# The last expert item of a mixture-of-experts layer taken out of the matmul engine's loop, its scatter products placed between its last products, and the gathered rows added on GpSimd

## What is computed

```
logits = h @ router_w + router_b
top_v, top_i = top_k(logits, 2);  top_p = softmax(top_v)
for e in range(8):                          # D_FF_EXPERT = 2816
    out += gates[:, e:e+1] * ((silu(h @ w1[e]) * (h @ w3[e])) @ w2[e])
x = x + g2 * out
return rmsnorm(x, final_norm_w)
```

## Time and profile before

| | us |
|---|---|
| median of 3 runs | 1505.53 (1504.87 to 1506.3) |
| span of the profiled execution | 1505.1 |
| last item's main products end (chain of waits) | 1493.51 |
| last instruction ends, before the last store lands | 1502.03 |

### The profile page before, as it was taken

How to read it: one execution, slowest core, us unless ns; L and a number is a source line. 1 busy time by engine, 2 the same in 40 slices (tenths; PEclk the granted TensorE clock), 3 DMA queues, 4 the chain that set the end, 5 groups by cost and what they waited for, 6 DMA issues and landing times.

```text
span 1505.1 us, 24325 instructions
## 1 busy us (share of the span) xinstructions
PE 1490.6 (99%) x8505; PEld 1311.0 (87%) x8505; DVE 1299.7 (86%) x1529; ACT 959.8 (64%) x1107; POOL 26.7 (2%) x44
## 2 busy tenths in 40 slices
PE   8999999999999999999999999999999999999997
PEld 7999888999999999888988888888888888888886
DVE  7999787777775799787799999999999999999998
ACT  3636445444544535444588888887878878788885
POOL 0000000000000000000010000000000000000100
PEclk9999999999999999999999999999999999999999
DMA  9956498388995646588399999999999999999993
GB/s 349 341 173 221 151 331 293 103 291 297 377 410 193 210 154 218 174 291 306 109 398 397 410 394 404 372 379 409 363 392 369 382 406 364 393 369 379 411 393 139
DMA packets 210458, 470.89 MB, mean 313 GB/s; under 512 B 16156, under 2 KB 93140, under 8 KB 210388
## 3 DMA queue, kind: packets, MB, share of 16 engines
q1 hardware_dynamic: 206624, 457.27, 83.0%
q0 software_dynamic: 3488, 12.59, 2.1%
q10 hardware_dynamic: 276, 0.09, 0.0%
HBM read 454.69 MB, written 15.21 MB: 312 GB/s over the span
## 4 chain that ended last, share of the span: by engine, by line
PE 94%; DVE 3%; DMA 1%; ACT 0%; issue 0%; DVEq 0%; SPq 0%; ACTq 0%
PE psU L671 68%; PE psA L671 24%; DVE split L2046 1%; PE psA L1155 1%; DMA raw<-in_ada_w_dram 1%; PE psU L1115 0%; DVE adacc L1655 0%; PE psU L1068 0%; PE psA L747 0%; ACT split L1254 0%; DVE adacc L1652 0%; DVE work L1655 0%; DVE merged L1677 0%; DVE xT L2027 0%; DVE work L1652 0%
## 5 line engine op out<-in xcount | busy, mean ns | idle before, releaser
L1254 ACT ACTIVATE split<-raw 128x1024 fp32r<-128x1024 f32 x750 | 781.8, 1061 | 300.0 <-PE psU L671 134.3
L2046 DVE TENSOR_TENSOR split<-raw,split 128x1024 fp32r<-128x1024 f32 x528 | 617.2, 1221 | 22.8 <-ACT split L1254 10.4
L671 PE MATMUL psU<-split,yS 128*128 128x512 f32 x2448 | 564.6, 390 | 0.1
L671 PEld LDWEIGHTS psU<-split,yS 128*128 128x128 f32 x2448 | 458.0, 188 | 94.9 <-DVE split L2046 0.8
L671 PE MATMUL psU<-hS,split 128*128 128x256 f32 x2688 | 331.0, 285 | 0.1
L1507 DVE TENSOR_TENSOR split<-raw,split 128x1024 fp32r<-128x1024 f32 x222 | 264.2, 1219 | 77.3 <-ACT split L1254 76.5
L671 PEld LDWEIGHTS psU<-hS,split 128*128 128x128 f32 x2688 | 326.3, 193 | 1.5 <-issue 1.2
L671 PE MATMUL psA<-split,hidE 128*128 128x512 f32 x1056 | 246.0, 392 | 0.0
L671 PEld LDWEIGHTS psA<-split,hidE 128*128 128x128 f32 x1056 | 196.4, 188 | 40.2
L671 PE MATMUL psU<-split,hS 128*128 128x512 f32 x720 | 168.4, 391 | 0.0
L671 PEld LDWEIGHTS psU<-split,hS 128*128 128x128 f32 x720 | 134.3, 188 | 28.0 <-DVE split L1507 0.4
(11 more groups left out here) (267 smaller groups left out, 824.5 us busy)
## 6 DMA issues: line engine op xcount, KB each, us to landing
raw<-in_moe_w_dram SPq DMA_DIRECT2D x496, 512.0 KB, 5.8
raw<-in_w_in_dram SPq DMA_DIRECT2D x116, 512.0 KB, 6.0
raw<-in_ada_w_dram SPq DMA_DIRECT2D x96, 512.0 KB, 7.8
raw<-in_ffn_w_dram SPq DMA_DIRECT2D x66, 512.0 KB, 8.6
raw<-in_moe_w_dram SPq DMA_DIRECT2D x64, 256.0 KB, 6.2
raw<-in_w_o_dram SPq DMA_DIRECT2D x16, 512.0 KB, 5.5
token_rows<-sc SPq DMA_DIRECT2D x11, 512.0 KB, 13.0
raw<-in_w_br_a_dram SPq DMA_DIRECT2D x8, 512.0 KB, 6.6
```

What stands on the lines that cost most here:

```text
L671: return pe.matmul(o, a, b, start=start, stop=stop, skip_group_check=True)
L1254: return act.activation(o, i, ACT.Copy)
L2046: TTN(split[:, slot, 1, :], raw[:, (RAW0 + n) % RAW, :], split[:, slot, 0, :].bitcast(F32), ALU.subtract).then_inc(s_lo, 1)
```

## The change

1. **PE.** The loop body is a function `item(i, last)`. The loop runs over all items but the last, and the last is written out behind it. For it: no token rows are turned at w2 piece 8 (`s_gath` is raised by the first product of that piece, so ACT and DVE still copy what lies in psU 0 and 1); the gates are turned at w2 row 12 (`GATES_AT`) into psU 3; the last three w2 rows (19, 20, 21) are taken bank by bank, first three rows for half 0, then three for half 1, with scatter (tile 0, half 0) before the last row of half 1 and scatter (1, 0) behind it, then (0, 1) and (1, 1).
2. **DVE.** The four SCALAR_TENSOR_TENSOR are gone. `expert_rows(0)` waits for half 0's bank (`s_yb`), `expert_rows(1)` for the last piece. The additions of the scatter products wait for GpSimd's (`s_others`) and go half 0 of both tiles, then half 1 (`FINISH`). Behind the second, DVE waits for ACT's squares of half 0 and writes `fst[:, 4:6]` = sum / D + eps.
3. **ACT.** Squares of 128x512 in place of 128x1024; the root of a tile takes half 0's term as its bias.
4. **GpSimd.** Behind the four gathers it waits for them (`s_ygl`) and makes, four times, `yg = yg * prob` (tensor_scalar, 128x1024) and `oacc = oacc + yg` (tensor_tensor, 128x1024), each waiting for the one ahead.

The core of the diff:

```diff
+LAST_BY_BANK = NF - 3
+GATES_AT = 12
+FINISH = [(tt, half) for half in range(2) for tt in range(TT)]
...
+            pool.wait_ge(s_ygl, 64)
+            pool.wait_ge(s_prob, 2)
+            for k in range(2):
+                for tt in range(TT):
+                    c = 2 * k + tt
+                    link(pool.tensor_scalar(yg[:, c, :], yg[:, c, :], prob[:, c:c + 1], 0.0, ALU.mult, ALU.add))
+                    ins = pool.tensor_tensor(oacc[:, tt, :], oacc[:, tt, :], yg[:, c, :], ALU.add)
+                    if k == 0:
+                        link(ins)
+                    else:
+                        ins.then_inc(s_others, 1)
...
-            with pe.Fori(0, n_items) as i:
+            last_item = pe.value_load(nitem[0:1, 1:2], min_val=NE - 1, max_val=MAXI - 1)
+            def item(i, last):
...
+                            if last and n == GATHER_AT and (xs, ws) == (0, 0) and o is outs[0][0]:
+                                ins.then_inc(s_gath, 1)
...
-                    if n == GATHER_AT:
+                    if n == GATHER_AT and not last:
...
+                    if last and f == GATES_AT:
+                        pe.wait_ge(s_lastg, 2)
+                        turn_gates(psU[3]).then_inc(s_gate, 1)
+                    if last and f == LAST_BY_BANK:
+                        break
...
-            pe.wait_ge(s_xlo, n_items * 2 + 2)
-            pe.wait_ge(s_lastg, 2)
-            turn_gates(psU[0]).then_inc(s_gate, 1)
-            pe.wait_ge(s_gate, 2)
-            pe.wait_ge(s_yfirst, n_items)
-            scatter(0)
-            pe.wait_ge(s_ye, n_items + 1)
-            for j in range(1, 4):
-                scatter(j)
+                rows = list(range(LAST_BY_BANK, NF))
+                for half in range(2):
+                    for f in rows:
+                        slot = (NSPLIT + HID + f) % SPL
+                        if half == 0:
+                            pe.wait_ge(s_lo, i * NPC + (NSPLIT + HID + f + 1))
+                        elif f == rows[-1]:
+                            pe.wait_ge(s_xlo, i * 2 + 4)
+                            pe.wait_ge(s_gate, 2)
+                            pe.wait_ge(s_yfirst, i + 1)
+                            scatter(0, 0)
+                        for xs, ws in ((0, 0), (0, 1), (1, 0)):
+                            ins = mm(Y_BANKS[half][0:CAP, :], hidE[:, xs, f, :],
+                                     split[:, slot, ws, half * 512:(half + 1) * 512], False, f == NF - 1 and xs == 1)
+                        if half:
+                            ins.then_inc(s_used, 1)
+                    if half == 0:
+                        ins.then_inc(s_yb, 1)
+                scatter(1, 0)
+                pe.wait_ge(s_ye, i + 2)
+                scatter(0, 1)
+                scatter(1, 1)
...
-            for tt in range(TT):
-                act.wait_ge(s_add, 2 * tt + 2)
-                act.activation(work[:, 8 + tt, :], oacc[:, tt, :], ACT.Square, accum_out=vst[:, tt:tt + 1]).then_inc(s_a, 1)
...
+            for n, (tt, half) in enumerate(FINISH):
+                o = slice(half * 512, (half + 1) * 512)
+                act.wait_ge(s_add, n + 1)
+                act.activation(work[:, 8 + tt, o], oacc[:, tt, o], ACT.Square,
+                               accum_out=fst[:, 2 * half + tt:2 * half + tt + 1]).then_inc(s_fsq, 1)
+                if half:
+                    act.wait_ge(s_fsq, n + 1)
+                    act.wait_ge(s_fb, 1)
+                    act.activation(fst[:, 6 + tt:7 + tt], fst[:, 2 + tt:3 + tt], ACT.Sqrt, scale=1.0 / D,
+                                   bias=fst[:, 4 + tt:5 + tt]).then_inc(s_vst, 1)
...
-            dve.wait_ge(s_ygl, 64)
-            for k in range(2):
-                for tt in range(TT):
-                    c = 2 * k + tt
-                    link(STT(oacc[:, tt, :], yg[:, c, :], prob[:, c:c + 1], oacc[:, tt, :], ALU.mult, ALU.add))
-                settle()
+            dve.wait_ge(s_yst, n_items * 16)
+            dve.wait_ge(s_yb, 1)
+            expert_rows(0)
             dve.wait_ge(s_used, n_items * NPC + USED0)
-            dve.wait_ge(s_yst, n_items * 16)
-            expert_rows()
...
+            expert_rows(1)
+            dve.wait_ge(s_others, 2)
+            for n, (tt, half) in enumerate(FINISH):
+                dve.wait_ge(s_sct, n + 1)
+                o = oacc[:, tt, half * 512:(half + 1) * 512]
+                TTN(o, o, psU[2 * tt + half][:, :], ALU.add).then_inc(s_add, 1)
+                if n == 1:
+                    dve.wait_ge(s_fsq, 2)
+                    TS(fst[:, 4:6], fst[:, 0:2], 1.0 / D, EPS, ALU.mult, ALU.add).then_inc(s_fb, 1)
```

More of the change, by code:

```diff
@@ L328, in program @@
         stored = sb("stored", [P, 1])
+        fst = sb("fst", [P, 10])
         mx8 = sb("mx8", [P, 2, 8])
@@ L455, in program @@
         s_add = sem("scatter_added")
+        s_others = sem("gathered_rows_added")
+        s_yb = sem("last_item_first_bank_ready")
+        s_fsq = sem("final_half_squares_summed")
+        s_fb = sem("final_first_half_bias_ready")
         s_gate = sem("last_gates_turned")
@@ L1122, in turn_gates, with scatter @@
                 return last
-            def scatter(j):
-                tt, half = j // 2, j % 2
-                mm(psU[j][:, :], gwT[0:CAP, tt * P:(tt + 1) * P], ye[0:CAP, half * 512:(half + 1) * 512],
+            def scatter(tt, half):
+                mm(psU[2 * tt + half][:, :], gwT[0:CAP, tt * P:(tt + 1) * P], ye[0:CAP, half * 512:(half + 1) * 512],
                    True, True).then_inc(s_sct, 1)
@@ L1144, in piece @@
                         for o, k, cols, first, end in outs:
-                            last = mm(o, stationary(xs, k), split[:, (NSPLIT + n) % SPL, ws, cols],
-                                      first and xs == 0 and ws == 0, end and xs == 1)
-                    last.then_inc(s_used, 1)
+                            ins = mm(o, stationary(xs, k), split[:, (NSPLIT + n) % SPL, ws, cols],
+                                     first and xs == 0 and ws == 0, end and xs == 1)
+                            if last and n == GATHER_AT and (xs, ws) == (0, 0) and o is outs[0][0]:
+                                ins.then_inc(s_gath, 1)
+                    ins.then_inc(s_used, 1)
                 def turn(g):
@@ L1154, in turn @@
                     for m in range(len(GROUPS[g])):
-                        last = pe.transpose(T_BANKS[g % 2][:, m * CAP:(m + 1) * CAP],
-                                            sig[0:CAP, 2 + g % 2, m * P:(m + 1) * P], ident[0:CAP, 0:CAP])
-                    last.then_inc(s_turn, 1)
+                        ins = pe.transpose(T_BANKS[g % 2][:, m * CAP:(m + 1) * CAP],
+                                           sig[0:CAP, 2 + g % 2, m * P:(m + 1) * P], ident[0:CAP, 0:CAP])
+                    ins.then_inc(s_turn, 1)
                 def tokens(xs, k):
@@ L1202, in _ @@
                     n += 1
-            pe.wait_ge(s_xlo, n_items * 2 + 2)
-            pe.wait_ge(s_lastg, 2)
-            turn_gates(psU[0]).then_inc(s_gate, 1)
-            pe.wait_ge(s_gate, 2)
-            pe.wait_ge(s_yfirst, n_items)
-            scatter(0)
-            pe.wait_ge(s_ye, n_items + 1)
-            for j in range(1, 4):
-                scatter(j)
+                if not last:
+                    return
+                rows = list(range(LAST_BY_BANK, NF))
[13 more added lines that the diff above has]
+                        if half:
+                            ins.then_inc(s_used, 1)
+                    if half == 0:
[4 more added lines that the diff above has]
+                scatter(1, 1)
+            with pe.Fori(0, last_item) as i:
+                item(i, False)
+            item(last_item, True)
         @block.scalar
@@ L1479, in _ @@
             act.wait_ge(s_gate, 1)
-            copy(gwT[0:CAP, :], psU[0][0:CAP, 0:T]).then_inc(s_gate, 1)
-            for tt in range(TT):
-                act.wait_ge(s_add, 2 * tt + 2)
-                act.activation(work[:, 8 + tt, :], oacc[:, tt, :], ACT.Square, accum_out=vst[:, tt:tt + 1]).then_inc(s_a, 1)
-                step[0] += 1
-                act.wait_ge(s_a, step[0])
-                std(vst[:, 2 + tt:3 + tt], vst[:, tt:tt + 1], D).then_inc(s_vst, 1)
+            copy(gwT[0:CAP, :], psU[3][0:CAP, 0:T]).then_inc(s_gate, 1)
+            for n, (tt, half) in enumerate(FINISH):
[8 more added lines that the diff above has]
+                                   bias=fst[:, 4 + tt:5 + tt]).then_inc(s_vst, 1)
         @block.vector
@@ L2107, in _ @@
                 link(STT(picked[:, r, :], total[:, src, NO:], float(r + 1), ov[:, 5, :], ALU.is_equal, ALU.mult))
-            link(TS(nitem[:, :], total[:, src, 2 * NO - 1:2 * NO], float(NE), None, ALU.add))
+            for c in range(2):
+                link(TS(nitem[:, c:c + 1], total[:, src, 2 * NO - 1:2 * NO], float(NE - c), None, ALU.add))
             settle()
@@ L2170, in tokens_low, with expert_rows @@
```

(8 more changed lines are left out.)

9 lines of the change are left out of this document (2 added, 7 removed).

## The result

Median 1512.03 us (1511.8 to 1514.32, 5 runs) against 1506.3 for the kernel before (5 runs beside it): ratio 1.0042, 95% interval 1.0032 to 1.0053. The change makes the kernel slower: 5.7 us between the medians, 5 to 8 us by the interval.

What follows compares the result with a forecast made beforehand. PE, busy 99% of the span, was taken to bound the kernel, with DVE second to watch. Span 1505.1 - 0.2 (tail) + 7.0 = 1511.9, and 0.43 to the median: 1512.3 us, range 1504.7 to 1516.5.

Steps and rivals of the forecast that it cites:

- The large term: Last item: GpSimd's eight instructions hold DVE's low parts up at a shared read port, PE waits; +7.0 us, 4.5 to 10.8.
- rival (a): Last item: GpSimd and DVE read side by side, the eight instructions are hidden; 1505.3 us, chance 0.31.
- Where it began: Last item: GpSimd's eight start when the last gather lands, 9.3 us after its issue, at about 1425.8.
- Its prices: GpSimd in the last item: port held 0.92 us per tensor_scalar, 1.85 per tensor_tensor, 11.1 us together.
- Its parts on PE: Last item: PE stands 5.7 us for low parts, plus 1.3 for DVE's next two pairs of 128x512.
- some ten: Sign in the new profile: PE waits for "DVE split" about ten times between 1430 and 1455, 0.5 to 2 us each.
- Tail: After the main products: all the reordering saves about 0.2 us, 0.7 at most, or loses 0.5 with slower hand-overs.
- new wait: Tail: DVE's small bias instruction waits about 0.8 us for both of ACT's squares, third and fourth additions queued behind it.
- the last step: Tail: tile 0's root comes no earlier than before; from its final product, at 1498.9, DVE is the limit in both kernels.
- Code behind the loop: PE's written-out last item is fetched for the first time; taken as 0, bounds 0 and +0.6 us.
- From the span to the median: Whole run: the median of the runs stands 0.43 us over the profiled span.
- Rival (b): Last item: DVE goes first, GpSimd gets in only where DVE's queue is empty; 2 to 5 us, say 1508.8, chance 0.14.

Runs made afterwards that it cites:

- e1: Changed kernel with GpSimd's eight instructions left out, so the gathered rows are not added; 1506.22 us, last item's start to tile 0's final product 98.33 us.
- e9: Changed kernel with each of GpSimd's eight instructions cut in four of 256 columns; 1508.47 us, last item's start to tile 0's final product 100.07 us.
- e8: Changed kernel with GpSimd's pairs waiting for DVE's low parts: piece 28, piece 50, and two for the last; 1508.77 us, ratio 1.0012.
- e10: Changed kernel with GpSimd adding only the first rank's two pairs, at pieces 28 and 50, and DVE the second rank's; 1506.68 us, ratio 1.0003.
- e11: Changed kernel with all four GpSimd pairs let go at piece 50 of the last item; 1511.53 us in one run.

## Why the prediction was right

- **The large term.** +7.0 us forecast, 6.87 measured (e1 against the changed kernel), by the mechanism that was named: low parts of 2 to 3.4 us, PE waiting for "DVE split". The step that stood on the weakest evidence, that GpSimd's turn holds DVE for its own length, is shown by the rows 2.06 and 3.42, and the rival (a), no clash, is out. The evidence was weaker than I wrote: one gather of the kernel before, which I left out, ran beside a low part (that of 1413.24) and was not lengthened:

```profile
1413.27 0.94 POOL L644 DMA_INDIRECT work<-expert_rows,rowi  x1 [0.30 <-issue]
```

- **Where it began.** GpSimd began at 1425.6 against a forecast 1425.8, but counted from the item's start that is 27.05 us in place of 25.5: the gather took 10.84 us to land where I had 9.3, and the item began earlier. The match is chance.
- **Its prices.** The tensor_scalar holds 0.85 us (0.92 taken), the tensor_tensor 2.2 (1.85 taken). The estimate of 2.25, worked out from what the Trainium skill gives in "GPSIMD Engine Reference", section 3 (4497 ns for 2048 columns), was the better one: the hold is 2.2, the undisturbed length 2.4. The held time was thus 3.4 + 8.8 = 12.2 and not 11.1, and still the total was hit: the first tensor_scalar ran in DVE's gap ahead of 1426.86, and part of the first tensor_tensor beside two DVE instructions with an input in PSUM, so 10.7 us reached the low parts. I had allowed for neither. Two errors of over 1 us cancel.
- **Its parts on PE.** For the halts by low parts I had 5.7 us, and they come to 6.2; the pairs of 128x512 that were to add 1.3 behind them added nothing where they stand (1452 and 1458), and 0.6 came at the last hidden rows. Of "some ten" waits, spaced from 1430 to 1455, the profile shows three for low parts, 1.2 to 1.7 us, and one for `sig` near 1470.
- **Tail.** To the start of tile 0's final product -0.07 us was forecast (1498.9 for 1498.97) and -0.38 measured in e1; to the end of the last instruction -0.2 and -0.63. The predicted new wait of DVE for the squares is there, 0.80 us. But the last step does not quite hold. The root of tile 0 does come earlier, 97.74 us behind the item's start in e1 (98.10 before), and DVE is the limit from there only in the new order: in the kernel before its second tile began 0.36 us behind the end of the first, at 1500.61, in e1 0.12 us.
- **Code behind the loop** costs nothing that shows: e1 has it.
- **From the span to the median** I added 0.43 us; the profiled execution here had 1.6 us over its span. Against that the last item began 1.72 us earlier than in the trace of before. These cancel in part too. The forecast 1512.3 against 1512.03 is closer than its steps were.
- **Rival (b),** DVE goes first, is wrong for the changed kernel, but see below.

## What to carry to other kernels

An engine that looks idle is not free if its instructions hold up those of one that is nearly full: here, work on GpSimd that reads SBUF cost DVE most of its length (0.85 of 1.12 us, 2.2 of 2.4) where it met DVE instructions with two SBUF inputs. Before moving such work, add up its held time and set it against the other engine's idle time and its lead, at every place where the critical engine takes something from it: the smallest lead counts, and here it was not at the low parts (e9). Inside that budget the work was free (two pairs, or four tensor_scalars), and beyond it up to two thirds of it reached the critical engine. When the last root, reciprocal and product bind the tail, reordering what feeds them brings little.

## What was not expected of the hardware

In e8 a tensor_scalar of GpSimd sat through seven low parts in a row, each at its usual distance of 1.14 us, and ran only when DVE came to an instruction with an input in PSUM:

```profile
1469.15 8.91 POOL L664 TENSOR_SCALAR work<-work,prob 128x1024 f32<-128x1024 f32 x1
```

```profile
1475.85 1.21 DVE L2100 TENSOR_TENSOR split<-raw,split 128x1024 fp32r<-128x1024 f32 x1
1476.99 0.69 DVE L2225 TENSOR_TENSOR yS<-psU,yS 128x512 fp32r<-128x512 f32 x1
```

In e10 the same instruction took 8.91 us again, at the same distance from the item's start, 66.84 us. In e11, let go at the same piece (66.42 us behind the item's start), it took 3.14 and held DVE as everywhere else. So who goes first is not always settled by turns; what decides it is left open. It also means that e8 and e10 had the tensor_scalar of their second pair for nothing by a pattern that I did not plan, and that their pacing may not carry over. The tensor_tensor behind it held DVE as elsewhere:

```profile
1478.19 3.44 DVE L2100 TENSOR_TENSOR split<-raw,split 128x1024 fp32r<-128x1024 f32 x1
```
